# Two attentions of a transformer kernel: the softmax scale moves from the weights to the outputs, and VectorE copies every fourth set of turned blocks

## What is computed

```python
s = jnp.einsum('bqkgd,bskd->bkgqs', q_blk, k_blk) * scale + bias
s = jnp.where(valid, s, NEG)
p = jax.nn.softmax(jnp.concatenate([s, sink_l], axis=-1), axis=-1)[..., :SPAN]
return jnp.einsum('bkgqs,bskd->bqkgd', p.astype(v_blk.dtype), v_blk)
```

## Time and profile before

| | |
|---|---|
| runs, median (lowest to highest) | 1914.92 us (1914.68 to 1914.97) |
| profiled execution, its own time | 1917.37 us |
| span from its first to its last instruction | 1915.6 us |
| busy over the span | PE 1897.8, PEld 1567.2, DVE 964.2, ACT 772.1, POOL 182.8 us |
| mean granted clock of TensorE | 0.997 |
| first attention, first scores to last product | 84.2 to 154.8 us |
| second attention, the same | 673.1 to 740.0 us |

### The profile page before, as it was taken

One profiled execution on the slowest core, in us unless ns is written; L12 is line 12 of the kernel. 1 busy time (PEld: TensorE's weight loads), 2 busy tenths in 40 slices (PEclk: granted clock), 3 DMA queues, 4 the chain that ended last, 5 costly groups with the idle time before them and its releaser, 6 DMA issues.

```text
span 1915.6 us, 25105 instructions
## 1 busy us (share of the span) xinstructions
PE 1897.8 (99%) x10458; PEld 1567.2 (82%) x10458; DVE 964.2 (50%) x1497; ACT 772.1 (40%) x1251; POOL 182.8 (10%) x196
## 2 busy tenths in 40 slices
PE   9999999999999999999999999999999999999998
PEld 7878888888888867888888888878887888888887
DVE  5693665553245284566553236443655555425523
ACT  5494433333333295433333334233764443212321
POOL 4112200000005031300000103000000020000000
PEclk9999999999999999999999999999999999999999
DMA  6512233334333311232233332331112323233222
GB/s 191 197 35 77 80 97 99 99 92 141 93 104 123 99 41 56 89 98 92 97 99 91 102 105 99 99 106 61 59 38 86 116 90 97 99 99 96 93 97 88
DMA packets 54136, 182.96 MB, mean 96 GB/s; under 512 B 6604, under 2 KB 10060, under 8 KB 53512
## 3 DMA queue, kind: packets, MB, share of 16 engines
q1 hardware_dynamic: 51528, 172.28, 28.2%
q0 software_dynamic: 2352, 9.02, 1.6%
q10 hardware_dynamic: 144, 0.06, 0.0%
HBM read 176.58 MB, written 4.76 MB: 95 GB/s over the span
## 4 chain that ended last, share of the span: by engine, by line
PE 88%; ACT 5%; DVE 5%; issue 1%; DMA 1%; SPq 0%; DVEq 0%; ACTq 0%
PE bank L1903 22%; PE bank L1904 22%; PE bank L1905 22%; PE bank L1922 2%; ACT prob_long L848 2%; PE bank L1923 2%; PE bank L1924 2%; ACT pt_short L837 1%; PE bank L2153 1%; PE bank L1683 1%; PE bank L1686 1%; PE bank L1691 1%; PE bank L1981 1%; PE bank L1982 1%; PE bank L1983 1%
## 5 line engine op out<-in xcount | busy, mean ns | idle before, releaser
L1155 DVE TENSOR_TENSOR w_lo<-w_raw,w_hi 128x1024 fp32r<-128x1024 f32 (+3 forms) x319 | 388.6, 1220 | 712.3 <-ACT w_hi L661 711.9
L661 ACT CAST w_hi<-w_raw 128x1024 fp32r<-128x1024 f32 (+3 forms) x319 | 322.0, 1010 | 555.0 <-DMA w_raw<-in_w_down 132.4
L1903 PE MATMUL bank<-h_hi,w_hi 128*128 128x512 f32 x1272 | 497.1, 391 | 0.8 <-DVE w_lo L1155 0.5
L1904 PE MATMUL bank<-h_lo,w_hi 128*128 128x512 f32 x1272 | 496.1, 390 | 0.0
L1905 PE MATMUL bank<-h_hi,w_lo 128*128 128x512 f32 x1272 | 495.9, 390 | 0.0
L1903 PEld LDWEIGHTS bank<-h_hi,w_hi 128*128 128x128 f32 x1272 | 239.5, 188 | 53.1 <-issue 2.2
L1905 PEld LDWEIGHTS bank<-h_hi,w_lo 128*128 128x128 f32 x1272 | 239.5, 188 | 50.2
L1904 PEld LDWEIGHTS bank<-h_lo,w_hi 128*128 128x128 f32 x1272 | 239.5, 188 | 49.5
L1903 PE MATMUL bank<-a_hi,w_hi 128*128 128x512 f32 (+1 forms) x676 | 261.5, 387 | 0.0
L1904 PE MATMUL bank<-a_lo,w_hi 128*128 128x512 f32 (+1 forms) x676 | 261.3, 387 | 0.0
L1905 PE MATMUL bank<-a_hi,w_lo 128*128 128x512 f32 (+1 forms) x676 | 261.3, 386 | 0.0
(11 more groups left out here) (328 smaller groups left out, 2551.6 us busy)
## 6 DMA issues: line engine op xcount, KB each, us to landing
w_raw<-in_w_gu SPq DMA_DIRECT2D x87, 512.0 KB, 3.5
w_raw<-in_w_mlp_in SPq DMA_DIRECT2D x32, 512.0 KB, 3.5
w_raw<-in_w_mlp_out SPq DMA_DIRECT2D x32, 512.0 KB, 3.6
w_raw<-in_w_down SPq DMA_DIRECT2D x32, 448.0 KB, 3.3
w_raw<-in_w_out SPq DMA_DIRECT2D x24, 512.0 KB, 3.6
w_raw<-in_w_down SPq DMA_DIRECT2D x16, 512.0 KB, 3.5
w_raw<-in_w_gates SPq DMA_DIRECT2D x16, 512.0 KB, 3.4
w_raw<-in_w_qk_b SPq DMA_DIRECT2D x14, 512.0 KB, 3.7
```

Of the source, the lines that this page charges most:

```text
L661: nc.scalar.copy(hi_of(v), raw_of(v)).then_inc(w_hi_done, 1)
L1155: nc.vector.tensor_tensor(lo_of(v), raw_of(v), hi_of(v).bitcast(F32), ALU.subtract).then_inc(w_split, 1)
L1903: mm(acc, w1, hi, start=start, stop=False)
L1904: mm(acc, w1, lo, start=False, stop=False)
```

## The change

In the first two attentions the probabilities are no longer scaled. TensorE turns the exponentials themselves (its turn waits for `p_exp` in place of `p_ready`). When the last step of a pair has its sums, VectorE takes the eight reciprocals (four steps, two halves) in one instruction and spreads each over 64 columns of `raw`. TensorE turns these too, with eight more transposes, behind the turn of the first step of the next pair, into the upper half of banks 4 and 5; after the last step there is one more such turn. ScalarE copies both halves of the banks then, 1024 columns. When the pair's product is done, VectorE multiplies the bank by the turned reciprocals into `act_out`, rounds that to `h_hi` and takes the remainder from it; ScalarE's output copy is gone. VectorE also copies the turned blocks of the third step of each pair (d % 4 == 2), which ScalarE skips. The dilated attention (`phase` 2) keeps its way.

```diff
+        def turned_blocks(phase, d, steps):
+            begin, end = 0, 2 * len(steps[d].blocks) if d < len(steps) else 4
+            if phase < 2 and d and d % 4 == 0:
+                begin, end = 0 if d < len(steps) else 4, 8
+            return begin, end
+        def by_vector(phase, d, steps):
+            return phase < 2 and d < len(steps) and d % 4 == 2
...
             def copy_turned(phase, d, steps):
+                if by_vector(phase, d, steps):
+                    turned[0] += 1
+                    return
...
-                        if 0 <= s - LAG_V[phase] < n:
-                            copy_output(phase, s - LAG_V[phase], steps, o_hi)
...
+                    if phase < 2:
+                        dve.wait_ge(pt_copied, turned[0] + d + 2)
+                        dve.wait_ge(pv_done, pv[0] + d + 1)
+                        o = act_out[:, st.pair_no % 2, :]
+                        nc.vector.tensor_tensor(o, acc, pt_of(phase, d + 1)[:, 4 * P:8 * P], ALU.mult).then_inc(o_scaled, 1)
+                        dve.wait_ge(o_scaled, o_count[0])
+                        nc.vector.tensor_copy(o_hi[:, st.pair, :], o).then_inc(o_hi_done, 1)
+                        dve.wait_ge(o_hi_done, o_count[0])
+                        nc.vector.tensor_tensor(o_lo[:, st.pair, :], o, o_hi[:, st.pair, :].bitcast(F32),
+                                                ALU.subtract).then_inc(o_ready, 1)
+                        return
...
+                    d = s - LAG_T[phase]
+                    if 0 <= d < n and by_vector(phase, d, steps):
+                        dve.wait_ge(pv_done, pv[0] + d - 1)
+                        dve.wait_ge(t_ready, turned[0] + d + 1)
+                        m = 2 * len(steps[d].blocks)
+                        dst = pt_of(phase, d)[:, :P * m].rearrange("p (n r q) -> p r n q", n=m, r=2)
+                        src = turn_banks[:, :, :64 * m].rearrange("p r (n q) -> p r n q", n=m)
+                        nc.vector.tensor_copy(dst, src).then_inc(pt_copied, 1)
...
-                        nc.vector.reciprocal(rden[:, i, :], total).then_inc(rden_done, 1)
-                        for half in range(2):
-                            part = prob_of(phase, d, half)[:, :steps[d].width]
-                            nc.vector.tensor_scalar(part, part, rden[:, i, half:half + 1], None, ALU.mult).then_inc(p_ready, 1)
+                        if phase < 2 and steps[d].last:
+                            dve.wait_ge(p_exp, expd[0])
+                            of = steps[d].pair_no % 2
+                            nc.vector.reciprocal(rden[:, :, :], sums[:, :, :, of]).then_inc(rden_done, 1)
+                            rdens[0] += 1
+                            dve.wait_ge(rden_done, rdens[0])
+                            spread = rden[:, :, :].rearrange("p i (h o) -> p (i h) o", o=1).to_broadcast([P, 8, HD])
+                            nc.vector.tensor_copy(raw[:, of, :].rearrange("p (n d) -> p n d", n=8), spread).then_inc(roots_spread, 1)
...
+                if phase < 2 and d and d % 4 == 0:
+                    pe.wait_ge(roots_spread, heads[0] + d // 4)
+                    for i in range(4):
+                        for part in range(2):
+                            last = nc.tensor.transpose(ps[4 + part][:, 256 + 64 * i:256 + 64 * i + 64],
+                                                       raw[rows(part), (d // 4 - 1) % 2, P * i:P * i + P],
+                                                       ident[rows(part), 64 * part:64 * part + 64])
```

More of the change, by code:

```diff
@@ L833, in copy_turned @@
                 act.wait_ge(t_ready, turned[0] + 1)
-                n = 2 * len(steps[d].blocks)
-                dst = pt_of(phase, d)[:, :P * n].rearrange("p (n r q) -> p r n q", n=n, r=2)
-                src = turn_banks[:, :, :64 * n].rearrange("p r (n q) -> p r n q", n=n)
+                begin, end = turned_blocks(phase, d, steps)
+                dst = pt_of(phase, d)[:, P * begin:P * end].rearrange("p (n r q) -> p r n q", n=end - begin, r=2)
+                src = turn_banks[:, :, 64 * begin:64 * end].rearrange("p r (n q) -> p r n q", n=end - begin)
                 nc.scalar.activation(dst, src, ACT.Copy).then_inc(pt_copied, 1)
@@ L1332, in softmax @@
-                        nc.vector.reciprocal(rden[:, i, :], total).then_inc(rden_done, 1)
-                        rdens[0] += 1
-                        dve.wait_ge(rden_done, rdens[0])
-                        for half in range(2):
-                            part = prob_of(phase, d, half)[:, :steps[d].width]
-                            nc.vector.tensor_scalar(part, part, rden[:, i, half:half + 1], None, ALU.mult).then_inc(p_ready, 1)
+                        expd[0] += 2
+                        if phase < 2 and steps[d].last:
[6 more added lines that the diff above has]
+                            nc.vector.tensor_copy(raw[:, of, :].rearrange("p (n d) -> p n d", n=8), spread).then_inc(roots_spread, 1)
+                        elif phase == 2:
+                            dve.wait_ge(p_exp, expd[0])
+                            nc.vector.reciprocal(rden[:, d % 4, :], sums[:, d % 4, :, 0]).then_inc(rden_done, 1)
+                            rdens[0] += 1
+                            dve.wait_ge(rden_done, rdens[0])
+                            for half in range(2):
+                                part = prob_of(phase, d, half)[:, :steps[d].width]
+                                nc.vector.tensor_scalar(part, part, rden[:, d % 4, half:half + 1], None, ALU.mult).then_inc(p_ready, 1)
@@ L2061, in turn @@
                     wait_reads((act_read, 0, 0))
-                if not 0 <= d < len(steps):
+                if not (0 <= d < len(steps) or phase < 2 and d == len(steps)):
                     return
-                blocks = steps[d].blocks
                 if turned[0]:
                     pe.wait_ge(pt_copied, turned[0])
-                for half in range(2):
+                for half in range(2 if d < len(steps) else 0):
+                    blocks = steps[d].blocks
                     ready[0] += 1
-                    pe.wait_ge(p_ready, ready[0])
+                    pe.wait_ge(p_exp if phase < 2 else p_ready, ready[0])
                     first_key = steps[d].pieces[0][half]["first_key"]
@@ L2134, in softmax @@
                         pe.wait_ge(pt_copied, copied[0])
-                        banks = 1 if phase == 2 else 2
-                        if st.first and st.pair_no >= banks:
-                            pe.wait_ge(o_ready, heads[0] + st.pair_no - banks + 1)
+                        if st.first and phase < 2 and st.pair_no >= 2:
+                            pe.wait_ge(o_scaled, heads[0] + st.pair_no - 1)
+                        elif st.first and phase == 2 and st.pair_no:
+                            pe.wait_ge(o_ready, heads[0] + st.pair_no)
                         n_v = len(st.vs[0])
```

39 lines of the change are left out of this document (16 added, 23 removed).

## The result

| | median | lowest to highest | runs |
|---|---|---|---|
| changed kernel | 1942.45 us | 1941.59 to 1942.65 | 4 |
| kernel before, same chip | 1914.80 us | 1913.26 to 1914.97 | 4 |

The ratio is 1.0145, with a 95% interval of 1.0128 to 1.0163. Measured a second time (e10) it was 1.0140 (1.0123 to 1.0156). The forecast was 1935.4, so it had the side and the mechanism, and was 7 us short.

A forecast was written before the change was run, and what follows sets the result against it. TensorE, with 0.2 us of window slack, was taken to limit any gain, and new stalls to add time: 10.1 first attention, 8.5 second, 1.4 ends, 0.5 first pair, +20.5 on 1914.9 = 1935.4 us; range 1926 to 1943.

The forecast's parts named there:

- TensorE bounds what can be gained: Window pairs: TensorE's own work is 6.96 of 7.18 us, so no more than 0.2 us can come back.
- The burst: VectorE, first step of the next pair: reciprocal, spread, product, rounding and remainder in a row, 2.30 us where 1.33 stood.
- The moved copy: VectorE's copy of a pair's third turn, ahead of the fourth: 0.68 us for 512 columns, 0.95 for 768.
- the bound by the scaling's rate: Lower end for the moved copy, 0.49 us for 512 columns; the sum would be 3 to 4 us smaller.
- The stall at the fourth turn: TensorE waits once a pair for VectorE's copy of the third turn: 1.41 us window, 1.48 grid, 1.75 memory.
- The eight transposes: TensorE's added turn of the spread reciprocals, once a pair: 0.24 to 0.34 us, taken as 0.28.
- The stall on the long copy: ScalarE copies 1024 columns of the turn with roots in 1.06 us, which stalls TensorE 0.2 us more.
- The distances: Time per pair after the change: window 8.85 us, window to memory 8.59, memory 8.11, grid 7.92.
- The rivals below no change: Nothing to measure: TensorE alone decides, 1914 us, chance 0.11. Faster: grid and memory pairs gain, 1909 us, chance 0.09.
- slower by more: Rival: slow spread, later reciprocal and longer roots, 1941 us; GpSimd waits on the grid add 3.6; no chance of its own.
- The grid pairs of before: Second attention before the change: three grid pairs in 20.73 us, 6.91 each, so +1.01 a pair.
- The first pair of the window: Start of the first attention: this pair pays roots and the long copy, 0.5 us.

The follow-up runs named there:

- e10: The changed kernel as it is, measured once more beside the kernel before on one chip: 1941.43 us, ratio 1.0140.
- e7: Changed kernel with ScalarE copying all turned blocks again and VectorE's rounding and remainder one round later: 1917.17 us, 1.0010 of the kernel before.
- e1: Changed kernel with ScalarE copying every step's turned blocks again, the burst of five VectorE operations kept: 1926.11 us.
- e2: Changed kernel with the rounding to h_hi and the remainder one round later on VectorE, behind the moved copy: 1923.90 us.
- e8: Changed kernel with twelve unused matmuls on TensorE in each stall, ahead of the wait at the fourth turn: 1939.37 us.
- e5: Changed kernel with GpSimd's table additions for the last three grid pairs cut to 8 columns of each piece: 1938.25 us.
- e6: Changed kernel with two of the eight transposes of the spread reciprocals in most pairs, ScalarE's copy still 1024 columns: 1936.81 us.
- e3: Changed kernel with the spread of the reciprocals done twice, one more VectorE copy in each pair's burst: 1955.08 us.

## Why the prediction was right, and 7 us short

**TensorE bounds what can be gained** (slack of 0.2 on the window): right. With the burst split and the copy back on ScalarE, e7 has TensorE waiting 0.2 us in all from 100 to 160 us and is no faster than before.

**The burst**: 2.37 measured for 2.30, the spread at 0.43 and not at the bank operations' rate. **The moved copy** took 0.95 and 0.68 us, both as taken from the remainder's rate; the bound by the scaling's rate is out. That is also what the Trainium skill, VectorE: DVE Perf Modes, section Why PSUM operands drop a tier, says of copies that read a bank.

**The stall at the fourth turn**: 1.42, 1.51 and 1.77 us (151.09 - 148.78 - 0.54) for 1.41, 1.48 and 1.75. e1 and e2 took away either half of what stands ahead of it, and either gave back 16 to 19 us. **The eight transposes**: 0.25 for 0.28. **The stall on the long copy**: 0.1 for 0.2.

**The distances**: 8.86 for 8.85 on the window, 8.60 for 8.59 where it ends, 8.11 (e8) for 8.11, 7.89 to 7.93 (e5) for 7.92. The rivals below no change fall with these.

**What was missing, the clock.** The table's sum holds for a TensorE at full speed, and no term asked what a stall does to it. Against e8, the changed kernel's distances are longer by 1.28 (147.88 to 157.27), 0.78 and 0.96 in the second attention, and by 0.24 and 0.56 from VectorE's product for the seventh pair to TensorE's last product of the two attentions; that is 3.8 us behind waits at the fourth turn. To this come 1.2 us ahead of the second attention's first output (from the turn that waited 0.71 us to the product 705.86 - 696.16 = 9.70, against 703.05 - 694.51 = 8.54), behind waits that the change didn't bring. In all 5.0 us, of two profiled runs. The medians give less: 3.1 and 2.1 us between the changed kernel and e8, and 0.6 for what the twelve matmuls cost on the window, so about 3 to 4. The profile of before has no wait of TensorE over 0.7 us in the second attention and a clock of 1.00 all through both, so no row there could price it; but a case for it could have stood among the rivals.

**What was named and left out of the sum, GpSimd.** The "slower by more" rival had 3.6 us for it. Measured, with the clock at 1.00 (e8), two grid pairs took 8.97 and 8.52 for 7.9: 1.6 us.

**What was mis-sized.** The grid pairs of before: the earlier trace rows is cut at ScalarE's output copy, and that cut lies unevenly against VectorE's work. By the starts of the remainders the three distances are 6.80, 7.20 and 5.86, so 19.86 and not 20.73; the pairs of before were taken 0.9 us too long, and the loss on them that much too small. The first pair of the window cost 0.25 us for 0.5 (from the first scores to VectorE's first operation on the bank 103.84 - 84.01 = 19.83, against 103.80 - 84.22 = 19.58).

The sum then is 20.5 + 5.0 + 1.6 + 0.9 - 0.25 = 27.75. The two attentions are 27.1 us longer in the profile (from the first scores to the last product 82.58 for 69.93 and 80.68 for 66.25), the medians 27.6 apart. The 0.7 between sum and profile I leave open.

**The range.** 1942.45 lies 0.6 us under the upper end of 1943. That end was set for longer stalls in every pair or a slow spread; away from GpSimd the stalls were about as long as forecast, and the spread was fast. So side, place and size of the stall were right by their reasons, and that the missing clock term still fitted into the range was partly luck.

**Outside the attentions** little changed: the stretch between them is 0.8 us longer, and what follows them is 3.4 us shorter, so the two profiled spans differ by 24.2 us and the medians by 27.6. The 3.4 are a matter of the profiled run of before, which waited 2.4 us longer for weights around 1160 to 1200 us. Its row, then the changed kernel's:

```profile
ACT w_hi L661 <- DMA w_raw<-in_w_qk_dil: 18.0, 5, 6.7
```

```profile
ACT w_hi L672 <- DMA w_raw<-in_w_qk_dil: 15.6, 5, 4.9
```

Behind that wait the profile of before also has its clock at the lower level, where the changed kernel has 1.00:

```profile
1188.00:1190.00 2.00, 2.00 (x6) 1.52 (x6) 2.00 (x3) 0.71 (x1) 0.00 (x0) 0.50 0.00 0
1190.00:1192.00 2.00, 2.00 (x7) 1.52 (x6) 0.76 (x2) 0.00 (x0) 0.00 (x0) 0.50 0.00 0
```

Setting the sum on the median and not on that span was the right choice.

## What to carry to other kernels

Work that leaves a busy engine in small pieces and comes back in one piece can cost more than it weighs: ask what the piece stands ahead of, and sum the path from the first thing it delays to the next use of a buffer that exists once. Moving two operations one round later gave back 18.6 of 27.6 us with no work removed. And when a forecast has TensorE idle in one place for over a microsecond, add a case in which its clock falls behind it; in this kernel falls of the clock were 3 to 5 of the 27.6 us.

## What the runs showed of the hardware that I had not expected

- The granted clock of TensorE was at its lower level for 3 to 10 us behind some waits of 1.5 to 2.4 us (the 1.5 in e10, at 742 us), and for some 20 us behind one of 2.1 in e6 and one of 3.3 in e3. Other waits of 1.25 to 1.6 us had no fall behind them. The length of one wait doesn't decide it: the clock also fell in the changed kernel behind 0.39 and 0.71 us (697 us), in e1 behind 0.87 and 0.57 (710 us) and in e2 behind 0.65 and 0.94 (710 us), and in e10 it stayed at 1.00 behind the first of these pairs. Filling part of the gaps with matmuls whose result nobody uses kept it at 1.00. With the longer burst that made the program clearly faster (1944.65 against 1955.08); with the change's own, the medians are 3.1 and 2.1 us apart (1939.37 against 1942.45 and 1941.43) and the intervals overlap.
- One added VectorE copy of 0.34 us a pair cost 12.6 us with the gaps empty and 5.3 with them filled.
- A copy or rounding of 512 columns on VectorE took 0.57 to 0.87 us beside GpSimd's additions and 0.43 without; a product that reads a bank took 0.68 in both.
- In this kernel a matmul of scores or values in fp32 leaves two records in the trace, a transpose one: the twelve matmuls put into the stall have 24 and took 1.5 us; a product of three key blocks for two heads is six matmuls, has 12 and takes 0.80. Whoever counts matmuls by the trace and adds as many gets twice the time.
